# The first block's attention: values ahead of the next job's transposes, outputs ahead of the copies, D's columns turned behind the seventh scores

## The chip, the cores and the metric

The kernel runs on one core of a Trainium2 chip. The metric is the device time of one execution in microseconds. Five engines work side by side, each through its own list in order: PE (TensorE, matmuls and transposes), DVE (VectorE), ACT (ScalarE), POOL (GpSimd) and SP (SyncE, which here only issues DMAs). They wait for each other through semaphores. PE writes to PSUM, which has eight banks here: four called G, two called T (transposes) and two called A.

## The reference, cut to what matters

A transformer block of one kind (two layers), then a block of another kind (two layers), for 256 positions of width 1024, in float32. The change touches only the attention of the first block, which has four kinds of heads:

```
proj = rmsnorm(x) @ w_in                      # split into q, k, v of A, B, C, D
o_a  = dsa_attention(...)                     # top-64 keys per query by an index score, then softmax
o_b  = forgetting_attention(...)              # softmax with a learned decay
o_c  = differential_attention(...)            # two softmaxes per head, their difference times v
o_d  = sliding_window_sink_attention(...)     # window of 128 and a sink in the denominator
mix  = concatenate([o_a, o_b, o_c, o_d]);  x = x + rmsnorm(mix @ w_out)
```

Every softmax is probs = exp(logits - max) / sum, and the output is probs @ v.

## The kernel before

All matmuls with weights are made in three parts (high and low halves, in units of 512 rows by 512 columns): ACT makes the high half of a weight unit, DVE the low half (L1703). PE multiplies at L709, L710 and L716.

The attention of a layer is ten jobs, JOBS1: 0 is (B, tile 0), 1 (A, 0), 2 (B, 1), 3 and 4 (C, 0 and 1, first half), 5 and 6 (C, 0 and 1, second half), 7 (A, 1), 8 and 9 (D, 0 and 1). A tile is 128 queries; a job of tile 0 has 128 keys and one bank of turned probabilities, a job of tile 1 has 256 keys and two. A job goes through these steps:

- scores (`logits1`, PE, L871 and L875) into a pair of G banks;
- `prep` (DVE, L1764 and L1769): the maximum and its negative; for D also the sink (L1767, L1772);
- `exps` (ACT, L1234): the probabilities and their sums; releases the G banks for the job after next;
- `job_turn` (PE, L764): the probabilities are transposed into the two T banks in turn; each bank waits until the bank before last has been copied (semaphore s_tfree, one count for all copies in order);
- `copy_turned` (DVE, L1806): from T to PT, two buffers that alternate by job;
- `job_outputs` (PE, L823): probabilities times values into A; it waits for the job's copies and for the outputs of the job before last;
- `outputs` (DVE, L1815 to L1830): division by the sum; for C also lambda and the difference.

`run_jobs` exists on PE and on DVE. Round q of the loop (0 to 11) on PE makes the scores of job q, then the transposes of job q-1, then the values of job q-2; in round 10 the values stand ahead of the transposes. On DVE round q is the prep of job q, the copies of job q-1, the outputs of job q-2. The function `beside` puts other work in between. On PE: in round 0 half of the last projection chunk; in round 2 the transposes of C's columns and the other half, which ACT evacuates after C's columns (job 0's values need the same A banks and wait for that); in round 6, ahead of the scores of job 6, the transposes of D's columns (queries, and keys doubled), which wait until both copies of job 4 are done; in round 11 the transposes of the first half of the mixed columns. ACT copies D's columns after the exps of job 5. On DVE `beside` selects keys for job 7 in rounds 0, 1, 4 and 5 (L1951, L1953, then the mask, L1961), and in round 9 squares the outputs of C (L1999, L2001). Jobs of kind A wait for their mask. After round 11 the output projection starts on PE (unit U_OUT), once DVE has split the mixed columns (L1717).

Of the kernel before, what the change touches and what calls it, by code (L numbers as in the profile page):

```python
# [31 lines left out]
P = 128  # L32
# [22 lines left out]
D_Q, D_K, D_V = 2892, 3148, 3276  # L55
# [29 lines left out]
T_QK, T_JOB, T_MIX, T_N2, T_P, T_MLP, T_PX, TS1 = 4, 11, 30, 34, 38, 40, 56, 60  # L85
# [3 lines left out]
JOBS1 = [("B", 0, 0), ("A", 0, 0), ("B", 1, 0), ("C", 0, 0), ("C", 1, 0), ("C", 0, 1), ("C", 1, 1),  # L89
         ("A", 1, 0), ("D", 0, 0), ("D", 1, 0)]  # L90
Q_TURN_C, Q_TURN_D = 1, 5
# [8 lines left out]
def job_banks(jobs, q):  # L100


    if jobs is JOBS2:
        return sum(2 * (m + 1) for _, m, _ in jobs[:q])
    between = 2 * (q >= Q_TURN_C) + 2 * (q >= Q_TURN_D)
    return sum(m + 1 for _, m, _ in jobs[:q]) + between


def job_end(jobs, q):

    return job_banks(jobs, q) + (2 if jobs is JOBS2 else 1) * (jobs[q][1] + 1)
# [117 lines left out]
def program(nc, a, out):  # L229
# [3 lines left out]
    with ExitStack() as ctx:  # L233
# [134 lines left out]
        s_tfree = Tally(sem("s_tfree"), (TS1, TS2), credit=2)  # L368
# [10 lines left out]
        s_prope = Tally(sem("s_prope"), (4, 0))  # L379
# [320 lines left out]
        def _(pe):  # L700
# [98 lines left out]
            def job_outputs(blk, L, q, jobs, t0):  # L799

                kind, m, x = jobs[q]

                pe.wait_ge(s_tfree.sem, s_tfree.at(blk, L, t0 + job_end(jobs, q)))
                if jobs is JOBS1 and q == 0:

                    pe.wait_ge(s_evac.sem, s_evac.at(0, L, CH1))

                pe.wait_ge(s_o.sem, s_o.at(blk, L, q - 1))
                if kind == "E":
                    for h in range(2):  # L810
                        for g in range(3):
                            for kt in range(m + 1):
                                mm = nc.tensor.matmul(heads_out(q)[:, h * HD:(h + 1) * HD],  # L813
                                                      PT2[m][:, h, kt, g * P:(g + 1) * P],
                                                      ZV[:, kt, (g * HG + 2 * x + h) * HD:][:, 0:HD],
                                                      start=g == 0 and kt == 0, stop=g == 2 and kt == m)
                    mm.then_inc(s_pv.sem, 1)
                    return
                for u in range(4):
                    for kt in range(m + 1):  # L820
                        col = {"A": A_V + u * HD, "B": B_V + u * HD, "D": D_V + u // 2 * HD,
                               "C": C_V + (2 * (u // 2) + x) * HD}[kind]
                        mm = nc.tensor.matmul(A[:, q % 2, u * HD:(u + 1) * HD], PT[:, q % 2, kt, u * P:(u + 1) * P],  # L823
                                              Z[:, kt, col:col + HD], start=kt == 0, stop=kt == m)
                mm.then_inc(s_pv.sem, 1)
# [77 lines left out]
            def run_jobs(blk, L, jobs, t0, logits, probs, beside=None):  # L903
                for q in range(len(jobs) + 2):
                    if beside:
                        beside(q, False)
                    if q < len(jobs):
                        logits(L, q)
                    if beside:
                        beside(q, True)  # L910
                    if q == len(jobs):

                        job_outputs(blk, L, q - 2, jobs, t0)
                    if 1 <= q <= len(jobs):
                        job_turn(blk, L, q - 1, jobs, t0, probs)
                    if q >= 2 and q != len(jobs):
                        job_outputs(blk, L, q - 2, jobs, t0)


            pe.wait_ge(s_xin, 32)  # L920
# [5 lines left out]
            for L in range(DEPTH):  # L926
# [8 lines left out]
                zb = lambda col: [Z[:, m, col:col + P] for m in range(TILES)]  # L935
                db = lambda col: [DUP[:, m, col:col + P] for m in range(TILES)]

                def turn_qk(t, *blocks):
                    for b in range(0, len(blocks), 2):
                        transposes(0, L, 0, T_QK + t + b // 2, sum(blocks[b:b + 2], []))  # L940
# [42 lines left out]
                def beside(q, logits_made):  # L983

                    if not logits_made:
                        if q == Q_TURN_D + 1:

                            pe.wait_ge(s_prope.sem, s_prope.at(0, L, 4))

                            pe.wait_ge(s_tfree.sem, s_tfree.at(0, L, T_JOB + job_end(JOBS1, Q_TURN_D - 1)))  # L990
                            turn_qk(T_JOB - T_QK + job_banks(JOBS1, Q_TURN_D) - 2, zb(D_Q), zb(D_Q + P), db(P), db(2 * P))
                    elif q == 0:
                        w_in_unit(6, 0, LAST1)

                        pe.wait_ge(s_evac.sem, s_evac.at(0, L, 6))
                    elif q == Q_TURN_C + 1:

                        pe.wait_ge(s_prope.sem, s_prope.at(0, L, 2))

                        pe.wait_ge(s_tfree.sem, s_tfree.at(0, L, T_JOB + job_end(JOBS1, Q_TURN_C - 1)))  # L1000
                        turn_qk(T_JOB - T_QK + job_banks(JOBS1, Q_TURN_C) - 2, zb(C_Q), zb(C_Q + P), zb(C_K), zb(C_K + P))
                        w_in_unit(6, 1, LAST1)

                        pe.wait_ge(s_tfree.sem, s_tfree.at(0, L, T_JOB + job_banks(JOBS1, Q_TURN_C)))
                    elif q == Q_TURN_D + 1:
                        pe.wait_ge(s_tfree.sem, s_tfree.at(0, L, T_JOB + job_banks(JOBS1, Q_TURN_D)))
                    elif q == len(JOBS1) + 1:

                        pe.wait_ge(s_o.sem, s_o.at(0, L, MIX_AB))
                        turn(0, L, 0, T_MIX, Z[:, :, MIX0:MIX0 + DM], UK)  # L1010
# [683 lines left out]
        def _(dve):  # L1694
# [104 lines left out]
            def copy_turned(blk, L, q, jobs, t0, dst):  # L1799

                kind, m, _ = jobs[q]
                w = 4 * P
                for kt in range(m + 1):
                    t = t0 + job_banks(jobs, q) + kt
                    dve.wait_ge(s_t.sem, s_t.at(blk, L, t + 1))
                    nc.vector.tensor_copy(dst[:, q % 2, kt, 0:w], T[:, t % 2, 0:w]).then_inc(s_tfree.sem, 1)  # L1806

            def outputs(blk, L, q, jobs):

                kind, m, x = jobs[q]  # L1810
                dve.wait_ge(s_pv.sem, s_pv.at(blk, L, q + 1))
                if kind == "D":
                    tt(ls[:, q, :], ls[:, q, :], es[:, q, :], ALU.add)
                    dve.drain()
                nc.vector.reciprocal(rl[:, q, :], ls[:, q, :])  # L1815
                dve.drain()
                src = A[:, q % 2, 0:4 * HD].rearrange("p (u d) -> p u d", d=HD)
                by = rl[:, q, :].unsqueeze(2).to_broadcast([P, 4, HD])
                if kind != "C":
                    dst = Z[:, m, MIX0 + MIXCOL[kind]:MIX0 + MIXCOL[kind] + 4 * HD].rearrange("p (u d) -> p u d", d=HD)  # L1820
                    tt(dst, src, by, ALU.mult).then_inc(s_o.sem, 1)
                    return
                odd = rl[:, q, :].rearrange("p (h m) -> p h m", m=2)[:, :, 1]
                ts(odd, odd, lam[:, L:L + 1], -1.0, ALU.mult, ALU.mult)
                dve.drain()
                both = CB.rearrange("p (u d) -> p u d", d=HD)
                tt(both, src, by, ALU.mult)
                dve.drain()
                two = CB.rearrange("p (h m d) -> p h m d", m=2, d=HD)
                tt(CO[:, m, :, :].rearrange("p (h x) d -> p h x d", x=2)[:, :, x, :], two[:, :, 0, :], two[:, :, 1, :], ALU.add).then_inc(s_o.sem, 1)  # L1830

            def run_jobs(blk, L, jobs, t0, dst, beside=None):
                for q in range(len(jobs) + 2):
                    if q < len(jobs):
                        prep(blk, L, q, jobs)
                    if q == Q_TURN_C + 1:

                        lo(blk, L, 0, U_OUT)
                    if 1 <= q <= len(jobs):
                        copy_turned(blk, L, q - 1, jobs, t0, dst)  # L1840
                    if q == len(jobs) + 1:
                        turn_lo(blk, L, 0, T_MIX, UK, XH, XL)
                    if q >= 2:
                        outputs(blk, L, q - 2, jobs)
                    if beside:
                        beside(q)

# [501 lines left out]
```

## Time and profile before

| | us |
|---|---|
| median of 3 runs | 1925.85 (1924.94 to 1926.24) |
| profiled execution | 1923.9 |
| its span, first to last instruction | 1921.4 |
| PE busy | 1867.4 (97%) |
| DVE busy | 1168.7 (61%) |
| ACT busy | 883.3 (46%) |
| POOL busy | 104.1 (5%) |

Busy shares are means over the whole kernel; the stage that is changed lies from about 92 to 153 us in layer 0 and from about 464 to 526 us in layer 1, and has to be read by itself. In a row of a timeline the first number is the start in microseconds, the second the duration up to the last result, and what stands in brackets is how long the engine had been idle and which instruction ended the wait. Instructions overlap at their ends, so the distance between two starts is the better price. PEclk is the clock granted to TensorE as a share of its full speed.

### The profile page before, as it was taken

The page shows a single profiled execution, that of the slowest core. Times are in us where ns is not written, and L with a number is a line of the kernel's source. Part 1 is how long each engine was busy: PE and PEld are TensorE (multiplying, and loading weights), DVE is VectorE, ACT ScalarE, POOL GpSimd, SP SyncE. Part 2 cuts the span into 40 slices and gives each one's busy share as a digit, 9 for nine tenths or more (in the row PEclk, how much of TensorE's full clock was granted, in tenths as well). Part 3 has the DMA queues.
Part 4 walks back from the last instruction along what each step waited for, and adds up shares of the span by engine and source line. Part 5 has one row for each costly group of instructions (what it writes and reads, how often), then busy time and mean ns, then how long its engine had stood idle before and what let it go on. Part 6 is the DMA issues. An engine that isn't in the chain of part 4 may idle for free.

```text
span 1921.4 us, 22445 instructions
## 1 busy us (share of the span) xinstructions
PE 1867.4 (97%) x9135; PEld 1537.9 (80%) x9135; DVE 1168.7 (61%) x1352; ACT 883.3 (46%) x1063; POOL 104.1 (5%) x129
## 2 busy tenths in 40 slices
PE   7989999999899999999999999999999999999997
PEld 5877888878778887888878878887888878878886
DVE  4787554757775547456566675556456566675445
ACT  5555444555454445344355434443344355434442
POOL 5220100021100000000000000000000000000000
PEclk9999999999999999999999999999999999999999
DMA  7415876553155556663555746564663555655562
GB/s 248 160 45 157 234 217 209 198 167 125 37 189 194 178 174 209 214 214 102 157 188 181 237 163 215 179 218 165 212 217 101 154 191 182 232 168 166 181 218 92
DMA packets 194613, 340.47 MB, mean 177 GB/s; under 512 B 9550, under 2 KB 59630, under 8 KB 194512
## 3 DMA queue, kind: packets, MB, share of 16 engines
q1 hardware_dynamic: 188944, 327.76, 52.1%
q0 software_dynamic: 5568, 11.30, 2.8%
q8 instruction: 72, 1.18, 0.2%
q14 instruction: 29, 0.24, 0.0%
HBM read 333.24 MB, written 5.77 MB: 176 GB/s over the span
## 4 chain that ended last, share of the span: by engine, by line
PE 86%; DVE 7%; DVEq 3%; ACT 3%; issue 1%; DMA 1%; SPq 0%; ACTq 0%
PE G L709 19%; PE G L710 19%; PE G L716 19%; PE T L764 5%; PE A L709 4%; PE A L710 4%; PE A L716 4%; PE G L726 2%; PE G L727 2%; PE G L732 2%; PE T L813 1%; DVE wlo L1703 1%; ACT arena L1234 1%; PE A L726 1%; PE A L732 1%
## 5 line engine op out<-in xcount | busy, mean ns | idle before, releaser
L1703 DVE TENSOR_TENSOR wlo<-raw,whi 128x2048 fp32r<-128x2048 f32 (+3 forms) x290 | 623.8, 2154 | 517.7 <-ACT whi L1234 517.6
L1234 ACT ACTIVATE whi<-raw 128x2048 fp32r<-128x2048 f32 (+3 forms) x290 | 521.3, 1800 | 520.0 <-PE G L716 453.2
L709 PE MATMUL G<-whi,XH 128*128 128x512 f32 (+1 forms) x1392 | 550.9, 396 | 1.2 <-DVE arena L1795 1.2
L710 PE MATMUL G<-whi,XL 128*128 128x512 f32 (+1 forms) x1392 | 540.9, 389 | 0.0
L716 PE MATMUL G<-wlo,XH 128*128 128x512 f32 (+1 forms) x1392 | 342.4, 388 | 0.0
L709 PEld LDWEIGHTS G<-whi,XH 128*128 128x128 f32 x1392 | 261.5, 188 | 55.1 <-issue 2.3
L710 PEld LDWEIGHTS G<-whi,XL 128*128 128x128 f32 x1392 | 261.6, 188 | 52.8 <-issue 1.9
L716 PEld LDWEIGHTS G<-wlo,XH 128*128 128x128 f32 x1392 | 260.8, 188 | 52.8
L764 PE MATMUL T<-ident,arena 128*128 128x128 f32 x804 | 113.3, 280 | 14.7 <-ACT arena L1234 9.9
L764 PEld LDWEIGHTS T<-ident,arena 128*128 128x128 f32 x804 | 93.8, 143 | 33.7 <-issue 12.6
L1234 ACT ACTIVATE arena<-T 128x512 f32<-128x512 f32 (+2 forms) x92 | 45.9, 549 | 157.3 <-PE T L764 157.3
L709 PE MATMUL G<-whi,MH 128*128 128x512 f32 x192 | 75.1, 391 | 0.0
L710 PE MATMUL G<-whi,ML 128*128 128x512 f32 x192 | 74.7, 389 | 0.0
L709 PE MATMUL A<-whi,MH 128*128 128x512 f32 x168 | 65.4, 389 | 0.0
L710 PE MATMUL A<-whi,ML 128*128 128x512 f32 x168 | 65.4, 389 | 0.0
L709 PE MATMUL A<-whi,XH 128*128 128x512 f32 (+1 forms) x160 | 61.4, 385 | 0.0
L710 PE MATMUL A<-whi,XL 128*128 128x512 f32 (+1 forms) x160 | 59.8, 375 | 0.0
L1234 ACT ACT_TABLE_LOAD x40 | 51.3, 1283 | 14.1 <-PE T L764 8.5
L2114 DVE TENSOR_TENSOR arena<-G,swap 128x1024 f32<-128x1024 f32 (+1 forms) x36 | 43.4, 1205 | 22.7 <-PE G L716 18.9
L1686 POOL DMA_DIRECT2D YH<-bias_rows x4 | 3.4, 851 | 938.4 <-PE T L764 763.3
L1234 ACT ACTIVATE XH<-T 128x512 fp32r<-128x512 f32 x48 | 27.2, 595 | 56.5 <-PE T L764 56.1
L1234 ACT ACTIVATE MH<-T 128x256 fp32r<-128x256 f32 (+1 forms) x74 | 30.8, 466 | 47.7 <-PE T L764 47.7
(253 smaller groups left out, 2347.9 us busy)
## 6 DMA issues: line engine op xcount, KB each, us to landing
raw<-in_w_in SPq DMA_DIRECT2D x110, 1024.0 KB, 7.5
raw<-in_w_mlp_up SPq DMA_DIRECT2D x32, 1024.0 KB, 5.2
raw<-in_w_mlp_down SPq DMA_DIRECT2D x32, 1024.0 KB, 5.7
raw<-in_w_ffn_gate SPq DMA_DIRECT2D x44, 512.0 KB, 4.1
raw<-in_w_ffn_up SPq DMA_DIRECT2D x44, 512.0 KB, 5.1
raw<-in_w_out SPq DMA_DIRECT2D x16, 1024.0 KB, 5.0
raw<-in_w_ret_proj SPq DMA_DIRECT2D x16, 1024.0 KB, 5.1
raw<-in_w_ffn_down SPq DMA_DIRECT2D x28, 512.0 KB, 3.6
```

The source lines that it names most:

```text
L709: nc.tensor.matmul(dst(m), hx[:, k0 + k, rows], hi[:, k, :], start=first and k == 0, stop=False)
L710: nc.tensor.matmul(dst(m), lx[:, k0 + k, rows], hi[:, k, :], start=False, stop=False)
L716: mm = nc.tensor.matmul(dst(m), hx[:, k0 + k, m * P:(m + 1) * P], lo[:, k, :], start=False, stop=last and k == kb - 1)
L726: nc.tensor.matmul(dst(m), hx[:, k0 + k, rows], hi[:, k, :], start=first and k == 0, stop=False)
L727: nc.tensor.matmul(dst(m), lx[:, k0 + k, rows], hi[:, k, :], start=False, stop=False)
L732: mm = nc.tensor.matmul(dst(m), hx[:, k0 + k, rows], lo[:, k, :], start=False, stop=last and k == kb - 1)
L764: tr = nc.tensor.transpose(T[:, t % 2, n * P:(n + 1) * P], src, ident[:])
L813: mm = nc.tensor.matmul(heads_out(q)[:, h * HD:(h + 1) * HD], PT2[m][:, h, kt, g * P:(g + 1) * P], ZV[:, kt, (g * HG + 2 * x + h) * HD:][: ...
L1234: return nc.scalar.activation(out_, in_, func, **kw)
L1686: pool.dma_start(BR[j % 2][:, 0:6, :].bitcast(F32), src).then_inc(s_br[j % 2].sem, 16)
L1703: tt(lo_, src, hi.bitcast(F32), ALU.subtract).then_inc(part_sem(blk, c, s_lo, s_lo1), 1)
L2114: tt(dst, pair(bank)[:, :, 0:cols], BIN[:, c % 2, 0:cols].unsqueeze(1).to_broadcast([P, TILES, cols]), ALU.add).then_inc(s_evac.sem, 1)
```

## The change

On PE a round now makes the values of job q-2 ahead of the transposes of job q-1, in every round. On DVE the outputs of job q-2 stand ahead of the copies of job q-1. D's columns are transposed after the scores of job 6 instead of ahead of them. The same instructions are issued; only their order and two waits move.

```
PE run_jobs
-                    if q == len(jobs):
+                    if q >= 2:
                         job_outputs(blk, L, q - 2, jobs, t0)
                     if 1 <= q <= len(jobs):
                         job_turn(blk, L, q - 1, jobs, t0, probs)
-                    if q >= 2 and q != len(jobs):
-                        job_outputs(blk, L, q - 2, jobs, t0)
PE beside
                     if not logits_made:
-                        if q == Q_TURN_D + 1:
-                            pe.wait_ge(s_prope.sem, s_prope.at(0, L, 4))
-                            pe.wait_ge(s_tfree.sem, s_tfree.at(0, L, T_JOB + job_end(JOBS1, Q_TURN_D - 1)))
-                            turn_qk(T_JOB - T_QK + job_banks(JOBS1, Q_TURN_D) - 2, zb(D_Q), zb(D_Q + P), db(P), db(2 * P))
-                    elif q == 0:
+                        return
+                    if q == 0:
...
                     elif q == Q_TURN_D + 1:
+                        pe.wait_ge(s_prope.sem, s_prope.at(0, L, 4))
+                        pe.wait_ge(s_tfree.sem, s_tfree.at(0, L, T_JOB + job_end(JOBS1, Q_TURN_D - 1)))
+                        turn_qk(T_JOB - T_QK + job_banks(JOBS1, Q_TURN_D) - 2, zb(D_Q), zb(D_Q + P), db(P), db(2 * P))
                         pe.wait_ge(s_tfree.sem, s_tfree.at(0, L, T_JOB + job_banks(JOBS1, Q_TURN_D)))
DVE run_jobs
-                    if 1 <= q <= len(jobs):
-                        copy_turned(blk, L, q - 1, jobs, t0, dst)
                     if q == len(jobs) + 1:
                         turn_lo(blk, L, 0, T_MIX, UK, XH, XL)
                     if q >= 2:
                         outputs(blk, L, q - 2, jobs)
+                    if 1 <= q <= len(jobs):
+                        copy_turned(blk, L, q - 1, jobs, t0, dst)
```

## Rows read from the trace of the kernel before

**Rows 1.** The page: chain that ended last, share by engine.

```profile
PE 86%; DVE 7%; DVEq 3%; ACT 3%; issue 1%; DMA 1%; SPq 0%; ACTq 0%
```

**Rows 2.** Windows: busy us (instructions) by engine, attention stage of both layers.

```profile
92.00:153.00 61.00, 55.15 (x427) 48.09 (x426) 51.29 (x115) 30.32 (x98) 12.58 (x16) 0.97 0.17 53
464.00:526.00 62.00, 55.67 (x432) 48.73 (x432) 51.19 (x115) 30.80 (x99) 12.76 (x16) 0.97 0.16 52
```

**Rows 3.** Timeline, PE, layer 0: start, duration, operation, [idle before <-releaser].

```profile
109.55 0.66 PE L764 MATMUL T<-ident,arena 128*128 128x128 f32 x4 [0.52 <-ACT arena L1234]
110.45 1.08 PE L823 MATMUL A<-arena 128*128 128x64 f32 x8 [0.24 <-issue]
...
122.78 1.06 PE L764 MATMUL T<-ident,arena 128*128 128x128 f32 x8 [1.70 <-DVE arena L1806]
...
133.57 1.09 PE L764 MATMUL T<-ident,arena 128*128 128x128 f32 x8 [0.32 <-ACT arena L1234]
134.50 1.90 PE L823 MATMUL A<-arena 128*128 128x64 f32 x16
136.33 1.14 PE L871 MATMUL G<-arena 64*128 64x256 f32 x8
...
140.66 1.10 PE L823 MATMUL A<-arena 128*128 128x64 f32 x8 [0.47 <-DVE arena L1806]
142.12 3.76 PE L764 MATMUL T<-ident,arena 128*128 128x128 f32 x16 [0.35 <-ACT arena L1234]
145.71 1.90 PE L823 MATMUL A<-arena 128*128 128x64 f32 x16
147.42 0.48 PE L709 MATMUL G<-whi,XH 128*128 128x512 f32 x1
```

**Rows 4.** Timeline of DVE, layer 0.

```profile
112.54 0.69 DVE L1764 TENSOR_REDUCE mx<-G 128x4 f32<-128x512 f32 x1 [0.30 <-PE G L875]
...
115.65 1.22 DVE L1764 TENSOR_REDUCE mx<-G 128x4 f32<-128x1024 f32 x1 [0.40 <-PE G L875]
...
117.03 0.68 DVE L1806 COPY arena<-T 128x512 f32<-128x512 f32 x1
117.83 0.18 DVE L1815 RECIPROCAL rl<-ls 128x4 f32<-128x4 f32 x1
...
126.86 1.22 DVE L1764 TENSOR_REDUCE mx<-G 128x4 f32<-128x1024 f32 x1
...
135.24 1.28 DVE L1806 COPY arena<-T 128x512 f32<-128x512 f32 x2
...
138.06 1.23 DVE L1764 TENSOR_REDUCE mx<-G 128x4 f32<-128x1024 f32 x1 [0.27 <-PE G L875]
...
139.92 0.69 DVE L1806 COPY arena<-T 128x512 f32<-128x512 f32 x1
...
141.28 0.69 DVE L1999 TENSOR_TENSOR arena<-gains 128x512 f32<-128x512 f32 x1
...
143.15 0.69 DVE L1806 COPY arena<-T 128x512 f32<-128x512 f32 x1 [0.17 <-PE T L764]
...
144.61 0.15 DVE L1813 TENSOR_TENSOR ls<-ls,es 128x4 f32<-128x4 f32 x1
```

**Rows 5.** Timeline of ACT, layer 0.

```profile
109.36 0.99 ACT L1234 ACTIVATE arena<-A,stat 128x332 f32<-128x332 f32 x2
...
140.04 0.20 ACT L1234 ACTIVATE es<-ds_ 128x4 f32<-128x4 f32 x1 [3.08 <-DVE ds_ L1772]
```

**Rows 6.** Timeline of POOL: last step of D's rotation, layer 0.

```profile
117.08 1.27 POOL L692 TENSOR_TENSOR arena<-arena,gains 128x512 f32<-128x512 f32 x1
```

**Rows 7.** Half-microsecond windows, with the granted clock (PEclk).

```profile
142.50:143.00 0.50, 0.50 (x4) 0.50 (x3) 0.40 (x2) 0.50 (x1) 0.00 (x0) 0.50 0.00 0
...
514.50:515.00 0.50, 0.50 (x3) 0.50 (x4) 0.50 (x1) 0.50 (x1) 0.00 (x0) 0.50 0.00 0
```

**Rows 8.** Timeline of PE, layer 1: first output projection.

```profile
519.68 0.48 PE L709 MATMUL G<-whi,XH 128*128 128x512 f32 x1
```

## The prediction

> **What bounds the kernel now.** I read the page first, then the two attention stages engine by engine. The chain that ended last is 86% PE, with a tenth on DVE and its queue [rows 1]: outside the attention of the first block PE is never short of work, so a shift inside that stage travels to the end unchanged, once per layer. In the stage itself PE and DVE are both close to full: 55.15 and 51.29 us busy of 61 in layer 0, and 55.67 and 51.19 of 62 in layer 1, while ACT has half its time free [rows 2]. The reader should see that neither has an idle stretch into which a microsecond could vanish. In the PE timeline the stage has a few short waits: 1.70 us for DVE's copies before D's columns, 0.32 for the exps of job 7, 0.47 for a copy and 0.35 for the exps of job 9 [rows 3]. In the DVE timeline there are 0.30 and 0.40 us of waiting for scores of jobs 3 and 4 and 0.27 for those of job 9 [rows 4]. What counts as the stage's end is the first matmul of the output projection, at 147.42 in layer 0 [rows 3] and 519.68 in layer 1 [rows 8], 372.26 us apart. I work out layer 0 and take it twice.
>
> **The prices.** A bank of turned probabilities: two in 0.93 us (133.57 to 134.50), so 0.45 each. Values of a two-tile job 1.83 us (134.50 to 136.33); of a one-tile job 0.93, half of it and the wait-free part of its row of 1.10 [rows 3]. A DVE copy 0.60 us to the next instruction (two are 1.28 with their tail, one 0.68). The prep of a two-tile D job 1.86 us (138.06 to 139.92); of a one-tile D job 1.32, shorter by the reduction (1.23 against 0.69). Evicting the outputs of job 7: 0.76 us (139.92 to 141.28 less a copy) [rows 4]. For C, with two more small operations, I estimate 1.25; for D, with one more, 0.9.
>
> **Part 1, the second round (jobs 0 to 2).** Values of job 0 wait for the evacuation of the last projection chunk, which ends at 110.35 (0.99 from 109.36 [rows 5]); they start at 110.45. Before, the transposes of job 1 filled this wait at 109.55 [rows 3]. Now they stand behind the values and push the scores of job 3 by 0.45, so the prep at 112.54 becomes 112.98; its 0.30 of idle shows it had no slack [rows 4]. Price +0.45, which nothing covers: the nearest cover is the 0.40 of idle at 115.65, which is a wait for the same shifted PE.
>
> **Part 2, DVE's order (all jobs).** The copies need only transposes that are done early; the outputs need values that PE makes late. Job 3's copy ran at 117.03, exactly while DVE would have waited for job 2's values at 117.83 [rows 4]. Now DVE waits first and copies after: +0.6 on that copy, less what the 0.45 already covers in waits. I carry +0.65 into the prep of job 5. From there to job 8 DVE does the same work without a wait, so the shift stays at 0.6 to 0.65. Edit priced from both sides: 0 if the wait absorbs it, +0.60 if not; I take +0.2 above part 1.
>
> **Part 3, D's columns behind the seventh scores.** D's transposes wait for both copies of job 4, and those now stand behind job 3's outputs: 122.78 becomes 122.78 + 0.65 + 1.25 = 124.7. The scores no longer wait for them, so they are ready before 122.5. But their reader is DVE, which selects the top keys until the prep at 126.86 [rows 4]; before, the scores ended by 122.78 + 0.93 + 1.73 (start of D1's scores to the prep that reads them, the longest) = 125.4, already 1.4 early [rows 3, 4]. So the 1.70 of PE wait was hidden, and its removal is worth 0; the cover is the selection, and without it the edit would give up to 1.7. On the other side ACT's copies of D are no longer hidden by those scores, and the values of job 4 start some 1.0 later; DVE wants them only after the prep at 127.5, so 0 too. POOL's rotation of D ends at 118.35 [rows 6], and no DMA is issued or passed anywhere in this change.
>
> **Part 4, round 8.** Copies of job 6 now stand behind the outputs of job 5 and end where job 8's prep starts: 135.24 - 1.32 + 0.6 = 134.5 [rows 4]. Values of job 6 need them and start at 134.6, as before (134.50). But the transposes of job 7, done at 133.57 while PE waited, now come behind: the scores of job 9 start at 134.6 + 1.83 + 0.93 = 137.36 against 136.33 [rows 3]: +1.03. DVE gets there at the same moment (values ready 136.5, outputs 1.25, two copies 1.2: 139.0), so prep 9 starts at 139.1 instead of 138.06.
>
> **Part 5, the end of the stage.** Prep 9 is done at 140.95, the exps start at 141.1 (140.04 + 1.03 [rows 5]) and are done 2.1 later, at 143.2. Values of job 7 run 139.2 to 141.05; DVE evicts them until 141.75 and only then copies job 8, until 142.35, so the values of job 8 run 142.4 to 143.35, where they ran at 140.66 under the exps [rows 3]. The transposes of job 9 start at 143.35 against 142.12: +1.23. DVE first does the squares (1.7, from 141.28 to the wait before 143.15), to 144.1, then job 8's outputs to 145.0, which used to come at 144.61, after the copies of job 9 [rows 4]. So these copies are done at 145.6 and 146.2, the mixed columns follow each of them (146.3 + 0.45), and the values of job 9 end at 146.75 + 1.83 = 148.6 against 147.42. Sum at full clock: **+1.2 us**. DVE's subtraction for the mixed columns ends near 148.4, just under it.
>
> **The clock.** The 16 transposes at 142.12 took 3.6 us to the next row, where 4 banks at 0.45 are 1.8 [rows 3]; the granted clock is 0.50 at 142.5 in layer 0 and at 514.5 in layer 1 [rows 7], that is 1.2 of 2.4 GHz. Ahead of the fall PE had made the values of jobs 7 and 8 and idled only 0.47 and 0.35 us between them and behind them. If the same stretch is at half clock after, it meets job 8's values (+0.93) and job 9's transposes, part of it behind DVE's outputs: the end comes at 149.0, **+1.6**. The two ends are +1.2 and +1.6; I take 1.6, since the rows show the fall in both layers.
> The Trainium skill ("TensorE: Matmul & The Clock Gate", Part 1) says that the clock is throttled by default and that activity releases it, idleness bringing the throttle back. The trace agrees only in part: it fell behind much work and little idleness. By that rule the new gaps of 2.3 us ahead of D's columns and 1.0 ahead of job 8's values would each invite another fall; that is rival 1.
>
> **Sum.** 2 x 1.6 = 3.2 us. The profiled execution took 1923.9 us (span 1921.4), which makes 1927.1; the median of the runs is 1925.85, which makes **1929.0**. What a measurement here can tell from no change is 0.2%, 3.9 us.
>
> **Rivals.** (1) The clock falls once more per layer, for PE's work is now strung out: 2.3 us of waiting before 124.7, then 0.9 until ACT has copied D, 1.0 before 142.4. For it: the fall before came with shorter gaps. Against: the wait of 1.70 at 122.78 brought none; the eight transposes behind it took 1.06 us, full speed, where those at 142.12 took twice that each [rows 3]. A second fall costs what lies on the path, 0.4 to 1.8 per layer (1.8 is what the one of before took from PE): 1930 to 1933, say 1931.3. (2) No change: the end of the stage absorbs it, since the clock no longer falls there, or DVE's queue loses less than I add. Without any half clock the new order costs 1.2, and if part 4's 1.0 is absorbed after all, 0.2: 1925.85 + 2 x 0.2 = 1926.2, with a spread of 1925 to 1927.2. (3) Faster: freeing the scores of job 6 lets DVE go ahead. It gives up to 1.7 per layer, and decides only from the point where the selection ends before 125.4 instead of 126.86; with it the end moves off the stretch at half clock, half of whose 1.8 I count as lost before: 1925.85 - 2 x (1.7 + 0.9) = 1920.7. Against it: DVE shows no idle time at 126.86 [rows 4], and parts 4 and 5 would have to cost nothing. That the change does nothing at all is excluded: all three orders are written into the queues.
>
> **Chances.** Forecast 0.50 (its own range 1927.3 to 1930.3), rival 1 0.22, rival 2 0.20, rival 3 0.08. Slower by over 0.2% (above 1929.7): a third of the forecast and rival 1, 0.38. Within: 0.54. Faster: 0.08. Range 1925.2 to 1932.6.
>
> **What would show it.** Right: DVE's prep of job 5 about 0.65 late relative to the C copies, D's columns at about +1.9 behind a PE wait of over 2 us, prep 6 still straight behind the mask with no idle; the scores of job 9 about 1.0 late, job 8's values alone behind a wait of 1.0; the projection at 148.6 to 149.0, and the same 372 us later. Wrong: a prep 6 or 7 that starts earlier than 126.86, or a projection before 147.8; or stretches at half clock elsewhere, which would make rival 1.

## The result, and the profile after

The change made the kernel slower: 1942.55 us (median of 4 runs, 1940.97 to 1948.58) against 1926.05 us before in the same runs (1924.94 to 1927.68), a ratio of 1.0095 with a 95% interval of 1.0081 to 1.0110. I had forecast 1929.0 and a range up to 1932.6. The profiled execution took 1942.67 us, its span is 1940.6.

The page of the changed kernel says at once where to look. It shows the granted clock in 40 slices: in the third and the eleventh slice it is no longer 9.

```profile
PEclk9969999999899999999999999999999999999999
```

These two slices hold the attention of layers 0 and 1. The next rows are the windows from the first scores of a layer to its output projection, and the stretch between the two (length, busy us and instructions of PE, PEld, DVE, ACT, POOL, then granted clock, DMA share, GB/s).

```profile
92.98:161.06 68.08, 62.93 (x402) 54.41 (x401) 47.33 (x107) 30.39 (x98) 12.58 (x16) 0.75 0.15 47
477.75:539.05 61.30, 52.63 (x401) 45.18 (x401) 47.23 (x107) 30.29 (x98) 12.77 (x16) 0.92 0.17 53
161.06:477.75 316.69, 312.39 (x1456) 255.52 (x1456) 189.90 (x223) 159.24 (x187) 32.63 (x37) 1.00 0.63 191
```

Before, the same stretch is 55.2 us in layer 0 (scores at 92.20, projection at 147.42 [rows 3]) and 55.6 in layer 1 (464.07, 519.68 [rows 8]); now it is 68.1 and 61.3. That is 12.9 and 5.7 us, 18.6 of the 19.2 by which the span of the profiled execution grew (the medians differ by 16.5, since executions differ), and nothing else in the kernel moved by more than a microsecond. The mean clock tells how much of each stretch PE spent at 1.2 instead of 2.4 GHz: twice 0.25 of 68.08 is 34 us in layer 0 and twice 0.08 of 61.30 is 10 us in layer 1, where before it was 3.4 us per layer, one stretch each, of which [rows 7] show one window. Half-microsecond windows show the two edges in layer 0:

```profile
112.50:113.00 0.50, 0.50 (x6) 0.33 (x6) 0.42 (x2) 0.00 (x0) 0.45 (x1) 1.00 1.06 414
113.00:113.50 0.50, 0.50 (x8) 0.50 (x8) 0.50 (x2) 0.00 (x0) 0.41 (x1) 0.58 1.05 410
120.00:120.50 0.50, 0.50 (x6) 0.50 (x4) 0.09 (x1) 0.00 (x0) 0.00 (x0) 0.50 0.00 0
...
147.00:147.50 0.50, 0.50 (x6) 0.50 (x5) 0.27 (x1) 0.00 (x0) 0.00 (x0) 0.79 0.00 0
147.50:148.00 0.50, 0.50 (x7) 0.50 (x6) 0.43 (x1) 0.00 (x0) 0.00 (x0) 1.00 0.00 0
```

The clock falls at 113.1, 1.7 us after PE resumed from the wait ahead of job 0's values, and does not rise for 34 us. PE's own timeline around it, with the wait, three operations at half clock and, behind the rise, two waits of the end of the stage:

```profile
111.39 1.08 PE L823 MATMUL A<-arena 128*128 128x64 f32 x8 [1.57 <-ACT arena L1231]
...
115.91 1.92 PE L764 MATMUL T<-ident,arena 128*128 128x128 f32 x8
...
120.17 3.62 PE L823 MATMUL A<-arena 128*128 128x64 f32 x16
...
134.69 3.67 PE L823 MATMUL A<-arena 128*128 128x64 f32 x16 [0.69 <-ACT arena L1231]
...
155.06 1.10 PE L823 MATMUL A<-arena 128*128 128x64 f32 x8 [0.92 <-DVE arena L1803]
...
158.35 1.17 PE L764 MATMUL T<-ident,arena 128*128 128x128 f32 x8 [1.31 <-DVE arena L1803]
```

These answer to [rows 3]. The values of job 0 now stand behind a wait of 1.57 us, into which the transposes of job 1 used to fall at 109.55. From then on eight transposes take 1.92 us instead of 1.06, the values of a two-tile job 3.62 instead of 1.90. At half clock PE has hardly a wait left; it has become the engine that everybody waits for. DVE's timeline shows it, where [rows 4] had waits of 0.3 to 0.4 us:

```profile
120.41 1.23 DVE L1761 TENSOR_REDUCE mx<-G 128x4 f32<-128x1024 f32 x1 [1.85 <-PE G L875]
...
123.82 0.18 DVE L1812 RECIPROCAL rl<-ls 128x4 f32<-128x4 f32 x1 [1.94 <-PE A L823]
...
133.73 1.22 DVE L1761 TENSOR_REDUCE mx<-G 128x4 f32<-128x1024 f32 x1
...
138.40 0.18 DVE L1812 RECIPROCAL rl<-ls 128x4 f32<-128x4 f32 x1 [3.20 <-PE A L823]
```

The prep of job 6 stands straight behind the key selection as before, but at 133.73 instead of 126.86. The waits of the stage in total (engine and line, what for, us, times, longest):

```profile
DVE rl L1812 <- PE A L823: 9.3, 6, 3.2
...
DVE mx L1761 <- PE G L875: 5.3, 4, 1.9
```

In layer 1 the same wait of 1.55 us was there and the clock held; it fell at 512.4, in the second of the two waits around D's columns, for 6.9 us, and once more at 526.1 for 3.4 us, behind a wait of 1.31 us ahead of job 6's values:

```profile
496.28 1.07 PE L823 MATMUL A<-arena 128*128 128x64 f32 x8 [1.55 <-ACT arena L1231]
...
510.78 1.06 PE L764 MATMUL T<-ident,arena 128*128 128x128 f32 x8 [2.10 <-DVE arena L1803]
512.58 3.68 PE L823 MATMUL A<-arena 128*128 128x64 f32 x16 [0.74 <-ACT arena L1231]
...
523.76 2.00 PE L823 MATMUL A<-arena 128*128 128x64 f32 x16 [1.31 <-DVE arena L1803]
```

### The profile page after: what moved, and what is told of

It reads as the page before. It is cut to its first block, busy times and chain, and to the rows that moved or that the text cites. A ratio compares the mean times of both kernels' runs of the same rounds, so it can differ in the third digit from the quotient of the medians.

```text
span 1940.6 us, 22447 instructions
## 1 busy us (share of the span) xinstructions
PE 1884.9 (97%) x9135; PEld 1550.9 (80%) x9135; DVE 1169.5 (60%) x1352; ACT 883.7 (46%) x1063; POOL 101.9 (5%) x129
## 4 chain that ended last, share of the span: by engine, by line
PE 87%; DVE 7%; DVEq 2%; ACT 2%; issue 1%; DMA 1%; SPq 0%; ACTq 0%
PE G L709 19%; PE G L710 19%; PE G L716 19%; PE T L764 5%; PE A L709 4%; PE A L710 4%; PE A L716 4%; PE G L726 2%; PE G L727 2%; PE G L732 2%; PE A L823 1%; PE T L813 1%; DVE wlo L1700 1%; PE A L726 1%; PE A L732 1%
## 5 line engine op out<-in xcount | busy, mean ns | idle before, releaser
L1700 DVE TENSOR_TENSOR wlo<-raw,whi 128x2048 fp32r<-128x2048 f32 (+3 forms) x290 | 623.9, 2154 | 518.0 <-ACT whi L1231 518.0
L1231 ACT ACTIVATE arena<-G,nm 128x128 f32<-128x128 f32 (+1 forms) x80 | 32.5, 418 | 44.4 <-DVE nm L1766 44.4
```

The lines of the kernel that those rows point to most:

```text
L1231: return nc.scalar.activation(out_, in_, func, **kw)
L1700: tt(lo_, src, hi.bitcast(F32), ALU.subtract).then_inc(part_sem(blk, c, s_lo, s_lo1), 1)
```

## The experiments

Two theories stood against each other. **L**: the new order opens waits in PE, the clock falls, and at half clock the attention's own work does not bring it back soon. **O**: the order costs its time by itself, through the waits between PE and DVE, and the clock only follows. Most experiments show the windows from first scores to output projection of both layers, with the clock in the third column from the right; they and the stretches at half clock are those of one profiled execution of each kernel. The runs were made in groups, each with its own executions of the kernel before (medians from 1924.01 to 1925.67 us), so ratios compare better than times. "Unused matmuls" are 256 columns wide, multiply parts of XH and write to a place that the next real matmul overwrites or nobody reads; they leave the computation as it is:

```
+            def warm(blk, L, q, n):
+                bank = G[:, 2, 0:256]
+                if q == 2:
+                    pe.wait_ge(s_exp.sem, s_exp.at(blk, L, 2))
+                else:
+                    pe.wait_ge(s_o.sem, s_o.at(blk, L, q - 3))
+                    bank = A[:, q % 2, 256:512]
+                for _ in range(n):
+                    nc.tensor.matmul(bank, XH[:, 0, 0:P], XH[:, 1, :], start=True, stop=True, skip_group_check=True)
```

**1. The wait ahead of job 0's values filled** (changed kernel):

```
 job_outputs
+                if jobs is JOBS1 and q == 0:
+                    warm(blk, L, 2, 12)
```

> The changed kernel plus 12 narrow-independent matmuls (fp32r, 256 columns, some 0.11 us each, result unused) that PE makes while it waits ahead of job 0's values, where the changed kernel idled 1.55 us in both layers. Theory L (latch): the fall of the granted clock at 113.3 us in layer 0 follows from that wait, and the attention's own work then never brings the clock back for 34 us. Without the wait the clock stays at 1.00 through the C jobs, layer 0's output projection comes 10 to 13 us earlier than in the changed kernel (161.1 to about 149 to 151), total 1930 to 1934. Theory O (order): values ahead of transposes and outputs ahead of copies cost their time through the waits between PE and DVE, and the clock only follows; then the extra matmuls change nothing: 1940 to 1943.

Measured: 1935.27 us (1935.0 to 1935.5), ratio to before 1.0049 (1.0034 to 1.0064).

```profile
92.00:152.23 60.23, 52.87 (x414) 45.71 (x413) 46.99 (x107) 30.26 (x98) 12.59 (x16) 0.94 0.16 53
468.87:530.34 61.47, 53.91 (x414) 46.82 (x413) 47.14 (x107) 30.27 (x98) 12.74 (x16) 0.92 0.15 52
108.00:126.00 18.00, 15.35 (x136) 12.96 (x135) 12.77 (x32) 8.91 (x31) 7.23 (x12) 1.00 0.19 59
```

```profile
125.38 1.06 PE L764 MATMUL T<-ident,arena 128*128 128x128 f32 x8 [2.11 <-DVE arena L1818]
127.18 3.19 PE L825 MATMUL A<-arena 128*128 128x64 f32 x16 [0.74 <-ACT arena L1246]
```

The stretch from 113 on is gone, and 7 us with it. Twelve matmuls that compute nothing made the kernel faster, which O can't explain. But it landed 1 us above L's range: the clock now fell at 127.7 for 6.8 us, behind the waits of 2.11 and 0.74 us at D's columns, and in layer 1 for 10 us in two stretches, as in the changed kernel.

**2. Round 2 in the old order** (changed kernel, the transposes of job 1 ahead of job 0's values in that round alone):

```
 run_jobs (PE)
-                    if q >= 2:
+                    if q >= 3 or (q >= 2 and jobs is not JOBS1):
                         job_outputs(blk, L, q - 2, jobs, t0)
                     if 1 <= q <= len(jobs):
                         job_turn(blk, L, q - 1, jobs, t0, probs)
+                    if q == 2 and jobs is JOBS1:
+                        job_outputs(blk, L, q - 2, jobs, t0)
```

> The changed kernel, but in round 2 alone PE makes the transposes of job 1 ahead of job 0's values, as before. Theory L: four transposes cut the wait of 1.55 us to about 0.5 and 0.25, the clock does not fall at 113, and the total is 1929 to 1934. Theory O: one round of ten is restored, so 1 to 2 us of 16 come back: 1939 to 1942.

Measured: 1938.03 us (1936.35 to 1940.55), ratio 1.0068 (1.0050 to 1.0085).

```profile
92.42:153.34 60.92, 52.85 (x401) 45.38 (x401) 47.05 (x107) 30.36 (x98) 12.60 (x16) 0.92 0.16 53
469.95:531.18 61.23, 52.81 (x402) 45.22 (x401) 47.21 (x107) 30.25 (x98) 12.75 (x16) 0.92 0.16 52
```

No fall at 113 here either. There are 10 us at half clock in each layer: one stretch in layer 0, from 125.5, behind the wait ahead of D's columns; two in layer 1, 6.8 us there and 3.4 us behind the wait of 1.32 us ahead of job 6's values. The total lies between the two expectations, 4 us above L's: L in the form that round 2 alone starts the trouble is too narrow.

**3. PE's order alone; 4. DVE's order alone; 8. both without D's move.** Applied to the kernel before, as in the change:

```
 run_jobs (PE), runs 3 and 8
-                    if q == len(jobs):
+                    if q >= 2:
                         job_outputs(blk, L, q - 2, jobs, t0)
...
-                    if q >= 2 and q != len(jobs):
-                        job_outputs(blk, L, q - 2, jobs, t0)
 run_jobs (DVE), runs 4 and 8
-                    if 1 <= q <= len(jobs):
-                        copy_turned(blk, L, q - 1, jobs, t0, dst)
...
                         outputs(blk, L, q - 2, jobs)
+                    if 1 <= q <= len(jobs):
+                        copy_turned(blk, L, q - 1, jobs, t0, dst)
```

> Only PE's order is changed (values ahead of transposes); DVE's order and D's columns as before. Theory L: the wait of round 2 is there, so the clock can fall at 113 in layer 0 and stay: 1936 to 1942. If the clock happens to hold, my working gives +0.9 per layer: 1928. Theory O with DVE's order as the costly part: 1926 to 1929 in all runs.

Measured: 1937.61 us (1930.97 to 1941.64), ratio 1.0063 (1.0042 to 1.0084).

```profile
91.83:153.94 62.11, 55.51 (x402) 48.04 (x401) 46.65 (x107) 30.25 (x98) 12.58 (x16) 0.86 0.15 52
470.54:536.75 66.21, 61.44 (x401) 52.90 (x401) 46.97 (x107) 30.36 (x98) 12.71 (x16) 0.77 0.14 49
```

> Only DVE's order is changed (outputs ahead of copies); PE's order as before. PE then waits for copies that stand behind outputs it makes itself only after its transposes. My working at full clock gives +3 per layer, 1932. Theory L: the wait of round 2 stays filled by the transposes, so no fall at 113 in layer 0; 1930 to 1936. Theory O: this is where most of the 16.5 us lie: 1936 to 1942.

Measured: 1944.33 us (1942.20 to 1945.55), ratio 1.0095 (1.0080 to 1.0110).

```profile
93.49:156.71 63.22, 54.41 (x402) 47.05 (x401) 47.30 (x107) 30.25 (x98) 12.58 (x16) 0.89 0.15 51
473.36:540.07 66.71, 57.04 (x401) 49.68 (x401) 47.58 (x107) 30.42 (x98) 12.72 (x16) 0.85 0.14 48
```

> The changed kernel without its third part: D's columns are transposed ahead of the scores of job 6 as before. Theory L: the wait of round 2 is there as in the changed kernel; the wait ahead of D's columns leads to half clock either way; 1936 to 1944. If D's move is what lengthens the half clock, layer 1's stretches at 512 and 526 go and the total is under 1936.

Measured: 1949.36 us (1938.89 to 1950.57), ratio 1.0112 (1.0082 to 1.0141).

```profile
91.88:160.15 68.27, 61.28 (x401) 52.71 (x401) 47.41 (x107) 30.39 (x98) 12.59 (x16) 0.78 0.15 47
476.76:544.67 67.91, 61.34 (x401) 52.93 (x401) 47.39 (x107) 30.38 (x98) 12.77 (x16) 0.77 0.15 48
```

Either part alone brings more half clock into both layers than the 3.4 us each of before: 17 and 31 us with PE's part, 14 and 20 with DVE's (and 4 more just after its second layer). PE's part alone ranges over 11 us from run to run, with mean clocks of 0.993 in its fastest and 0.986 in its slowest: one and the same order, different amounts of half clock. DVE's part alone lies above both ranges, and its clock fell where that order has PE wait 2.88 us for DVE's copies, not in round 2; run 12 tells what the order costs there by itself. Run 8 lies above L's range too. D's move is not what lengthened the half clock: without it both layers have 30 us of it, and the ratio is no better (the intervals overlap).

**7. D's move alone** (the change's hunk in `beside`, on the kernel before):

```
-                        if q == Q_TURN_D + 1:      # ahead of the scores of job 6
-                            turn_qk(..., zb(D_Q), zb(D_Q + P), db(P), db(2 * P))
                     elif q == Q_TURN_D + 1:        # behind them
+                        turn_qk(..., zb(D_Q), zb(D_Q + P), db(P), db(2 * P))
```

> Only D's columns are moved behind the seventh scores. My prediction's part 3: worth 0, 1925 to 1926.5 with the same stretch at half clock per layer. Theory L: the wait ahead of D's columns is now one piece of some 0.4 us more, or is split by the scores of job 6, so a fall at 125 us is possible in a layer and costs 1 to 3 us.

Measured: 1923.78 us (1921.67 to 1926.80), before 1924.01 in the same runs, ratio 0.9993 (0.9983 to 1.0003).

```profile
91.80:147.05 55.25, 49.49 (x401) 43.55 (x401) 46.46 (x107) 30.29 (x98) 12.61 (x16) 0.97 0.18 58
463.74:519.11 55.37, 49.52 (x402) 43.55 (x401) 46.48 (x107) 30.28 (x98) 12.76 (x16) 0.97 0.18 58
132.00:134.50 2.50, 2.50 (x18) 2.27 (x18) 2.06 (x6) 1.13 (x6) 0.00 (x0) 0.50 0.00 0
```

Worth nothing in the old order, as part 3 of the prediction had it for the new one. The stretch at half clock is as long as before, but begins at 131.6 instead of 142.3. It comes 1.6 us behind a wait ahead of job 6's transposes that the kernel before has too, at 130.34 and shorter. The rows are of this run and of the kernel before:

```profile
129.96 1.09 PE L764 MATMUL T<-ident,arena 128*128 128x128 f32 x8 [1.67 <-ACT arena L1233]
```

```profile
130.34 1.10 PE L764 MATMUL T<-ident,arena 128*128 128x128 f32 x8 [1.32 <-ACT arena L1234]
```

**5. All long waits filled** (changed kernel; 12 in round 2, 18 and 7 around D's columns, 10, 3 and 8 ahead of the values of jobs 6, 7 and 8, 10 ahead of the mixed columns):

```
 job_outputs
+                if jobs is JOBS1 and q + 2 in {2: 12, 8: 10, 9: 3, 10: 8}:
+                    warm(blk, L, q + 2, {2: 12, 8: 10, 9: 3, 10: 8}[q + 2])
 beside
+                        warm(0, L, q, 18)
                         turn_qk(..., zb(D_Q), zb(D_Q + P), db(P), db(2 * P))
+                        warm(0, L, q, 7)
...
+                        warm(0, L, 11, 10)
                         turn(0, L, 0, T_MIX, Z[:, :, MIX0:MIX0 + DM], UK)
```

> The changed kernel, with matmuls whose results are unused (256 columns, 0.11 us each) in every wait of PE longer than 0.7 us in the attention: 12 ahead of job 0's values, 18 ahead of D's columns and 7 behind them, 10 ahead of job 6's values, 3 and 8 ahead of those of jobs 7 and 8, 10 ahead of the mixed columns. Theory L (half clock is the price of the change): the clock stays at 1.00, and what is left is the order itself, 1.2 us per layer by my prediction's sum less the half clock that the kernel before has; total 1924 to 1929. Theory O: the new order costs more than that by itself; 1932 to 1940 with the clock at 1.00.

Measured: 1928.10 us (1926.89 to 1929.23), before 1924.01, ratio 1.0017 (1.0007 to 1.0026).

```profile
92.18:149.71 57.53, 56.09 (x470) 49.98 (x469) 46.81 (x107) 30.32 (x98) 12.60 (x16) 1.00 0.18 56
466.31:524.12 57.81, 56.08 (x469) 49.96 (x469) 47.03 (x107) 30.32 (x98) 12.77 (x16) 1.00 0.18 56
```

```profile
111.07 1.00 PE L825 MATMUL A<-arena 128*128 128x64 f32 x8
```

The clock is 1.00 in both layers, and of the loss 4.1 us are left, though PE has 68 matmuls more to make per layer. So about three quarters of the 16.5 us are half clock, and the rest is the order and what the extra matmuls overfill.

**6. Before, with its last two waits filled** (4 ahead of job 8's values, 3 ahead of job 9's transposes):

```
 job_outputs
+                if jobs is JOBS1 and q + 2 == 10:
+                    warm(blk, L, 10, 4)
 job_turn
+                if jobs is JOBS1 and q + 1 == 10:
+                    warm(blk, L, 11, 3)
```

> The kernel before, with 4 such matmuls in the wait ahead of job 8's values and 3 in that ahead of job 9's transposes. Theory L: the one stretch of 3.4 us at half clock per layer goes, which is worth 0.9 us each by the recurrence of my prediction: 0.5 to 2 us below before, 1923 to 1925. Rival: waits of 0.47 and 0.35 us have nothing to do with the fall, and the time is that of before or up to 0.5 us above.

Measured: 1926.78 us (1923.88 to 1931.18), before 1924.01, ratio 1.0011 (1.0000 to 1.0021): a miss.

```profile
93.65:152.23 58.58, 54.70 (x408) 48.13 (x408) 46.65 (x107) 30.37 (x98) 12.60 (x16) 0.88 0.17 55
...
124.00:138.00 14.00, 13.77 (x65) 11.50 (x65) 8.86 (x24) 4.21 (x17) 0.00 (x0) 0.51 0.01 1
```

```profile
124.23 1.94 PE L764 MATMUL T<-ident,arena 128*128 128x128 f32 x8 [1.71 <-DVE arena L1821]
```

The two small waits weren't it. In the profiled execution, the longest of the ten, the clock fell right behind the wait at D's columns, for 14 us, in layer 1 too (at 499.7). The kernel before has that very wait (1.70 us [rows 3]) and held its clock over it in its profile. So even the old order is exposed: its 25 runs in this comparison went from 1922.7 to 1929.2, the longer ones at a mean clock of 0.994 to 0.996 against 0.997.

**10. All filled but round 2** (run 5 without the entry `2: 12`).

> The changed kernel with the unused matmuls everywhere but in round 2, so that the wait of 1.55 us ahead of job 0's values stands. Theory L in its strict form: that wait alone starts the long stretch, and since at half clock the waits that the other matmuls fill are gone, nothing ends it until the D jobs, or until the 18 and 7 matmuls around D's columns, which then come at half clock and are dense work: 15 us instead of 34 in a layer where it falls; total 1932 to 1938. If the wait of round 2 doesn't matter: 1928, as with all of them.

Measured: 1935.52 us (1934.02 to 1937.00), ratio 1.0056 (1.0042 to 1.0069).

```profile
92.30:156.56 64.26, 62.11 (x458) 55.26 (x457) 47.01 (x107) 30.32 (x98) 12.58 (x16) 0.87 0.15 50
473.20:530.55 57.35, 54.57 (x458) 48.50 (x457) 47.09 (x107) 30.32 (x98) 12.74 (x16) 1.00 0.18 56
113.00:129.00 16.00, 16.00 (x84) 13.94 (x82) 9.23 (x24) 6.31 (x24) 5.05 (x9) 0.50 0.03 11
```

One kernel shows both cases: in layer 0 the clock fell behind the wait of round 2 and stayed down for 17 us, in layer 1 it held, and that layer is 6.9 us shorter. The total is within L's range, but the reason that I gave for the end of the stretch fell: it ended at 129.2, 1.3 us ahead of the extra matmuls at D's columns.

Now the wait ahead of job 0's values can be counted. Five profiled kernels have it at 1.5 to 1.6 us (the changed one, runs 3, 8, 10 and, next, 11). In 8 of their 10 layers the clock fell 0.5 to 1.7 us after its end. In the nine others, where it is filled or at most 0.54 us, the clock fell in round 2 in none of 18 layers.

**11. A burst of work inside the stretch** (changed kernel, in round 4):

```
 run_jobs (PE)
+                    if q == 4 and jobs is JOBS1:
+                        warm(blk, L, q, 24)
                     if q >= 2:
                         job_outputs(blk, L, q - 2, jobs, t0)
```

> The changed kernel with 24 unused matmuls of 256 columns in one piece in round 4, ahead of job 2's values, in both layers: 5.1 us at half clock, 2.7 at full. Theory L: in a layer where the clock has fallen in round 2, they bring it back to 1.00, and the stretch of 34 us ends near 120 to 125 us, though it may fall again at D's columns; extra work of 2.7 to 5 us per layer is paid for by 5 to 10 us of stretch: 1936 to 1943, with a first stretch of 7 to 10 us instead of 34. If the clock does not depend on the work in between: 1948 or more, and the stretch still lasts to 147 us.

Measured: 1949.22 us (1946.05 to 1950.82), ratio 1.0125 (1.0111 to 1.0139).

```profile
119.83 4.07 PE L912 MATMUL A<-XH 128*128 128x256 f32 x24
```

```profile
112.00:121.50 9.50, 9.50 (x50) 7.79 (x50) 5.78 (x10) 3.30 (x9) 5.82 (x10) 0.50 0.14 55
122.50:131.50 9.00, 7.88 (x72) 6.75 (x70) 5.14 (x16) 2.55 (x14) 0.00 (x0) 1.00 0.01 2
```

The clock rises in the middle of the burst, at 122.0 in layer 0 and at 507.7 in layer 1, and the first stretch is 10.2 us long in both. That fits theory L, but it does not show that the burst did it. The clock fell again, at 132.2 and at 518.0, and these stretches lasted 10.2 us as well, with no burst in them and with pauses:

```profile
132.50:142.00 9.50, 8.81 (x39) 7.13 (x40) 5.55 (x15) 3.12 (x10) 0.00 (x0) 0.50 0.00 0
```

In run 3 a stretch in the same place ended after 6.8 us without any. As a remedy the burst failed: the time is above my range, at the 1948 or more of the rival (whose stretch to 147 us did not come), and above the changed kernel's.

**9. and 12. At full clock, without and with DVE's part.** Run 9 is the old order with D's move and every wait of PE filled in rounds 2 to 11:

```
+FILL_VALUES = {2: 1, 10: 4}                     # round: count, ahead of the values
+FILL_TURNS = {2: 5, 5: 3, 7: 12, 8: 4, 10: 3}   # round: count, ahead of the transposes
+                        warm(0, L, q, 5)      # ahead of D's columns, and 6 behind them
+                        warm(0, L, 11, 4)     # ahead of the mixed columns
```

Run 12 adds DVE's hunk to it, and has 16 unused matmuls instead of 5 ahead of D's columns and 6 instead of 4 ahead of the mixed ones.

> The order of before with D's columns behind the seventh scores (as the run with that part alone), and unused matmuls in every wait of PE in rounds 2 to 11 (5 and 1 in round 2, 3 in round 5, 5 and 6 around D's columns, 12 in round 7, 4 in round 8, 4 and 3 in round 10, 4 ahead of the mixed columns). Theory L: no half clock in either layer, which by my recurrence is worth 0.9 us per layer, less up to 0.3 us where a wait is overfilled: 1922 to 1924, and a smaller spread than before's 6 us. Rival: the few us at half clock lie in waits anyway and cost nothing; 1924 to 1926.

Measured: 1923.34 us (1922.73 to 1924.41 in 11 runs), before 1925.55 (1921.73 to 1928.29), ratio 0.9991 (0.9982 to 1.0000).

```profile
92.21:147.49 55.28, 53.26 (x448) 47.95 (x448) 47.13 (x107) 30.32 (x98) 12.59 (x16) 1.00 0.18 58
464.09:519.83 55.74, 53.45 (x449) 47.93 (x448) 47.24 (x107) 30.32 (x98) 12.72 (x16) 1.00 0.19 58
```

> The kernel of the ninth run (waits of PE filled, D's columns moved), with DVE's outputs ahead of its copies as well, and 16 unused matmuls instead of 5 ahead of D's columns, 6 instead of 4 ahead of the mixed ones. PE keeps its transposes ahead of the values. It shows what DVE's part costs at full clock. By the recurrence of my prediction PE then makes values that wait for copies which DVE starts only after earlier outputs, 3.5 us per layer: 1929 to 1932, more than the changed kernel with its waits filled (1928.1), in which PE's part gives 1.5 per layer back. Rival: the two parts cost about the same, 1 us per layer each, and this comes at 1925 to 1926. Clock at 1.00 but for at most one stretch.

Measured: 1932.04 us (1931.41 to 1932.90), before 1925.67, ratio 1.0031 (1.0019 to 1.0042).

```profile
92.81:152.14 59.33, 55.66 (x461) 49.58 (x461) 46.88 (x107) 30.35 (x98) 12.61 (x16) 1.00 0.16 54
468.79:528.21 59.42, 55.65 (x462) 49.57 (x461) 47.01 (x107) 30.35 (x98) 12.74 (x16) 1.00 0.16 54
```

Run 9 has no half clock; the median is 2 us lower, with an interval that touches 1, so it is not shown to be faster than before, but its runs spread over 1.7 us instead of 6.6. Its windows are no shorter than those of run 7, the same order without the fill and with 3.4 us at half clock per layer (55.28 and 55.74 against 55.25 and 55.37), so one such short stretch has no cost to be seen here; run 9's fill starts job 0's values 0.3 us late, which may hide some. Run 12 has no half clock either, and its layers are 4.05 and 3.7 us longer: this is about what DVE's part costs by itself while PE keeps the old order, at the upper end of what I expected. So theory O is right for a part: in that order nearly 8 us of run 4's 20 are order. In the changed kernel PE's part gives some of it back (run 5: 57.5 and 57.8).

## Why the prediction was wrong

**Parts 1 to 5, the order at full clock: right in kind, a microsecond short per layer.** I had +1.2 us per layer at full clock. Run 5 against run 9 gives 57.53 - 55.28 = 2.25 and 57.81 - 55.74 = 2.07. Some of this is overfilled waits: in run 5 the values of job 0 start at 111.07 instead of 110.45, 0.6 late. I can't separate the rest. Part 3 (D's move worth 0) is confirmed by run 7 for the old order; in the new one, run 8 and the changed kernel can't be told apart. Part 5's "wait of 1.0" ahead of job 8's values is there in the changed kernel, at 155.06 with 0.92 us.

**The clock: the step that failed.** I took the half clock for a fixed stretch that might shift a little, priced it at +0.4 per layer, and priced its repetition (rival 1) at "0.4 to 1.8 per layer". Both prices come from what one such stretch had cost PE in the trace before. What the runs show instead is that a stretch has no fixed length: behind a wait the clock can fall, at half clock the same values and transposes run twice as long, and the clock stays down, for 3.4 us in one place and for 34 in another. The price isn't 1.8 us but 10.5 (layer 0 of the changed kernel against run 5: 68.1 - 57.5) for 34 us at half clock, and 3.5 (61.3 - 57.8) for 10 us in layer 1, both 0.3 us for each; in run 10 it is 6.9 us for 17, 0.4 each. These 14.0 us, for which my sum had 0.8, and the 4.3 of the order, for which it had 2.4, make up the 18.6 by which the two stages grew, within 0.3. My range held one more stretch of the old length per layer, and the changed kernel had ten times that length in layer 0.

**Part 1 named the wait and missed its weight.** I saw that job 0's values would now wait from the end of the projection chunk to 110.45 with nothing ahead of them, charged 0.45 us for the displaced transposes, and did not list the wait among the gaps for rival 1. It turned out to be the one with the longest stretch behind it. I listed the gap of 2.3 us at D's columns, and it is where the first falls of layer 1 and of runs 1 and 2 begin, and those of run 6 at its shorter form of before. My list of PE's waits in the trace before was short of one, the 1.32 us at 130.34; run 7, where it is 1.67, has its fall behind it.

**The rule of the Trainium skill** ("TensorE: Matmul & The Clock Gate", Part 1: throttled by default, released by activity) bears more than I gave it. Runs 5 and 9 agree with it, at 1.00 with their waits filled. That activity releases the throttle is not shown within a stretch: the rise in run 11's burst fits, but the stretches without a burst ended after the same 10.2 us, and in run 10 PE was busy for 16.00 of 16.00 us at a clock of 0.50. I gave the rule a chance of 0.22 since the fall before had come behind short waits. Its other half, that idleness brings the throttle back, agrees as a tendency: 8 of 10 layers fell behind the wait of 1.5 to 1.6 us in round 2, and none of 18 without it, but waits of 1.55 and 1.7 us came both with a fall and without.

**What stays open.** Why the clock falls behind the same wait in one layer and not in the other (the changed kernel and run 10), or in one kernel and not in the other (before and run 6), and what ends a stretch, after 3.4 us or after 34; no run here tells these apart.

## What to carry to other kernels

In a stage of many small matmuls, list every wait of PE that an edit opens or lengthens and look at the granted clock around it; a fall can last for 3 us or for half of the stage (34 of 68 us here), so the bad side of a range has to hold most of the stage at half clock. Work that falls into a wait, as job 1's transposes did, can be worth more than the 0.45 us that it hides: put back in run 2, they took the fall in round 2 away. Where such waits can't be avoided, unused matmuls in them kept the clock and steadied the time, but as a burst in the middle of real work they cost more than they brought.

## What the runs showed of the hardware that I had not expected

- PE at half clock can be busy without a pause for many microseconds and stay there: in run 10, 16.00 of 16.00 us busy at a clock of 0.50.
- The same kernel in the same order differs by 11 us from run to run (run 3: 1930.97 to 1941.64) together with its half clock, with mean clocks of 0.993 and 0.986; with the waits filled the spread is 1.7 us (run 9).
- 24 matmuls of 256 columns took 4.07 us across the rise of the clock in layer 0 (run 11), and the rise came 2 us after their start there and 3 us in layer 1.
- The wait of 1.5 to 1.6 us in round 2 was followed within 1.7 us by a fall in 8 of 10 profiled layers, and without it there was none in that round in 18.
